# Levels of a triangular inverse as 32x32 products on four row groups in place of 64x64 products on two quadrants

## The reference

```python
a_mat = jnp.where(strict, jnp.einsum('bhnik,bhnjk->bhnij', k_beta, k) * decay, 0.0) + jnp.eye(C, dtype=f32)
tri = functools.partial(lax.linalg.triangular_solve, left_side=True, lower=True, unit_diagonal=True)
u = tri(a_mat, v * beta[..., None])
w = tri(a_mat, k_beta * jnp.exp(g)[..., None])
```

## Time and profile before

| | us |
|---|---|
| three runs | 1550.43, 1552.90, 1553.49 |
| median | 1552.90 |
| the profiled execution | 1550.74 |
| its span in the trace | 1548.3 |

### The profile page before, as it was taken

The page is one execution under the profiler, slowest core; times in us unless marked ns, Lnnn a source line. Parts: engine busy times, 40 slices in busy tenths (PEclk is TensorE's granted clock), DMA queues, the critical chain, the costliest instruction groups (busy, mean ns, idle before and its releaser), DMA issues.

```text
span 1548.3 us, 24568 instructions
## 1 busy us (share of the span) xinstructions
PE 1446.0 (93%) x10321; PEld 1158.1 (75%) x10321; DVE 682.0 (44%) x1063; ACT 605.1 (39%) x872; POOL 572.3 (37%) x265
## 2 busy tenths in 40 slices
PE   7999899888769999999999799987999999999998
PEld 5787578777758788888888687754467888888886
DVE  4665676777554312213143405877823413132231
ACT  5525463434344423223133335467844313232231
POOL 5343231101023434343434332326944443434441
PEclk9999898999869999999999899998999999999999
DMA  4332110000113232323233222210012232223231
GB/s 141 95 96 68 55 28 3 3 3 3 57 43 95 82 109 82 109 82 106 84 101 90 67 83 69 82 55 1 1 55 83 98 93 93 97 86 104 83 106 55
DMA packets 128392, 110.00 MB, mean 71 GB/s; under 512 B 10678, under 2 KB 126512, under 8 KB 128304
## 3 DMA queue, kind: packets, MB, share of 16 engines
q1 hardware_dynamic: 127712, 107.64, 22.4%
q10 hardware_dynamic: 592, 1.07, 0.2%
HBM read 106.60 MB, written 2.10 MB: 70 GB/s over the span
## 4 chain that ended last, share of the span: by engine, by line
PE 78%; DVE 11%; ACT 5%; issue 3%; POOL 2%; DMA 1%; DVEq 0%; ACTq 0%; SPq 0%; POOLq 0%
PE ps L501 21%; PE ps L506 21%; PE ps L502 21%; PE ps L637 5%; DVE lower L1874 2%; DVE lower L1870 1%; POOL lower L2083 1%; PE ps L652 1%; PE ps L645 1%; PE ps L741 1%; ACT lower L1371 1%; PE ps L614 1%; PE ps L538 1%; PE ps L948 1%; DVE lower L1653 1%
## 5 line engine op out<-in xcount | busy, mean ns | idle before, releaser
L2051 POOL TENSOR_TENSOR w_lo<-lower,w_hi 128x2048 fp32r<-128x2048 f32 x84 | 387.4, 4612 | 637.2 <-ACT w_hi L1027 637.2
L501 PE MATMUL ps<-h_hi,w_hi 128*128 128x512 f32 x792 | 315.9, 399 | 8.9 <-ACT h_hi L1032 5.9
L502 PE MATMUL ps<-h_hi,w_lo 128*128 128x512 f32 x792 | 314.5, 397 | 0.0
L1027 ACT ACTIVATE w_hi<-lower 128x2048 fp32r<-128x2048 f32 x84 | 160.2, 1907 | 242.8 <-PE ps L506 242.8
L506 PE MATMUL ps<-h_lo,w_hi 128*128 128x512 f32 x792 | 201.6, 395 | 0.4
L502 PE MATMUL ps<-a_hi,w_lo 128*128 128x512 f32 x480 | 189.1, 394 | 0.0
L501 PE MATMUL ps<-a_hi,w_hi 128*128 128x512 f32 x480 | 189.1, 394 | 0.0
L501 PEld LDWEIGHTS ps<-h_hi,w_hi 128*128 128x128 f32 x792 | 150.3, 190 | 46.5 <-issue 11.5
L502 PEld LDWEIGHTS ps<-h_hi,w_lo 128*128 128x128 f32 x792 | 150.2, 190 | 36.0 <-issue 0.5
L506 PEld LDWEIGHTS ps<-h_lo,w_hi 128*128 128x128 f32 x792 | 148.7, 188 | 37.4 <-DVE h_lo L1576 1.8
L1819 DVE TENSOR_TENSOR lower<-lower,ps 128x512 f32<-128x512 f32 x64 | 44.0, 687 | 268.7 <-PE ps L506 268.7
(11 more groups left out here) (356 smaller groups left out, 1992.4 us busy)
## 6 DMA issues: line engine op xcount, KB each, us to landing
lower<-in_mlp_w_dram SPq DMA_DIRECT2D x64, 1024.0 KB, 5.4
lower<-in_ev_w_in_dram SPq DMA_DIRECT2D x30, 512.0 KB, 3.8
lower<-in_od_w_in_dram SPq DMA_DIRECT2D x10, 1024.0 KB, 5.0
lower<-in_ev_w_out_dram SPq DMA_DIRECT2D x4, 1024.0 KB, 5.1
lower<-in_od_w_out_dram SPq DMA_DIRECT2D x4, 1024.0 KB, 5.1
out_dram<-lower SPq DMA_DIRECT2D x4, 512.0 KB, 3.2
lower<-in_od_w_in_dram SPq DMA_DIRECT2D x6, 256.0 KB, 3.8
upper<-in_x_dram SPq DMA_DIRECT2D x1, 1024.0 KB, 7.8
```

The lines of the kernel that those rows point to most:

```text
L501: pe.matmul(o, wh, xh, start=(i_ == 0), stop=False)
L502: pe.matmul(o, wl, xh, start=False, stop=False)
L1027: act.activation(WH[:, u % 2, :, 0:w], RAW[:, u % 2, :, 0:w], ACT.Copy).then_inc(hi_ready, 1)
L2051: pool.tensor_tensor(WL[:, u % 2, :, 0:w], RAW[:, u % 2, :, 0:w], as_f32(WH[:, u % 2, :, 0:w]), ALU.subtract)\
```

## The change

A new helper, `quarters`, takes the place of `both_halves` in the two functions of the inverse's levels. For levels 0 to 3 it makes, for each head, four products of 32x32 by 32x32, one for each group of 32 partitions: rows i, output partitions i, with the diagonal 32x32 block of the head's matrix that lies there. These are 32 products per call. For level 4 it makes two products per head, one per chunk, 16 per call: for the product below, from rows 0 to 31 of a chunk to its output partitions 32 to 63, and for the joined one (`lower` False) from rows 32 to 63 to partitions 0 to 31. Each product starts and stops its own accumulation. The other calls of `both_halves`, the semaphores, the masks and the work of all other engines stay as they are.

```diff
+            def quarters(b, lev, mats, vals, lower):
+
+                for h_ in range(NH):
+                    j, q = h_ // 2, h_ % 2
+                    for i in range(4):
+                        here_ = i // 2 * 2
+                        if lev < LAST - 1:
+                            row, col, m_, n_ = i, i, i % 2, i % 2
+                        elif i % 2 == 0:
+                            row, col, m_, n_ = (here_, here_ + 1, 1, 0) if lower else (here_ + 1, here_, 0, 1)
+                        else:
+                            continue
+                        rows, cols = (slice(x * 32, x * 32 + 32) for x in (row, col))
+                        mm = pe.matmul(ps[cols, b, h_ * HD + n_ * 32:h_ * HD + n_ * 32 + 32],
+                                       mats[rows, j, q, m_ * 32:m_ * 32 + 32], vals[rows, j, q, n_ * 32:n_ * 32 + 32],
+                                       start=True, stop=True)
+                return mm
+
             def below_blocks(s, lev):
...
-                    both_halves(g, lt, ti, True).then_inc(inv_x, 1)
+                    quarters(g, lev, lt, ti, True).then_inc(inv_x, 1)
...
                     if lev < LAST - 1:
-                        both_halves(g, qi[s % 2], xm, True).then_inc(inv_y, 1)
+                        quarters(g, lev, qi[s % 2], xm, True).then_inc(inv_y, 1)
                     else:
-                        both_halves(g, xm, qi[s % 2], True).then_inc(inv_y, 1)
+                        quarters(g, lev, xm, qi[s % 2], False).then_inc(inv_y, 1)
```

## The result

| | before | after |
|---|---|---|
| median of the runs on one chip, us | 1552.8 | 1597.0 (1593.7 to 1601.2) |
| ratio, 95% interval | | 1.0295 [1.0265, 1.0325] |
| the profiled execution, us | 1550.7 | 1598.6 |
| its span, us | 1548.3 | 1596.6 |

The change costs 44 us by the medians and 48 us between the two profiled executions. The stage table of the kernel after (same columns as the earlier trace rows) says where: round 0, rounds 1 to 3, the last round, and everything behind the stage.

A forecast was written before the change was run, and what follows sets the result against it. TensorE was taken to bound levels 0 and 1 and the last level's end, DVE level 2 and much of level 3. Terms -3.8 - 9.3 + 4.2 = -8.9 us gave 1544 against the median; forecast 1538 to 1551, range to 1580.

The forecast's parts named there:

- the burst: After a stall, four matmuls and five weight loads of L629 started within 60 ns; taken as showing fast enough issue.
- g, the price of a group: One matrix kind of one level, below or joined: from 0.93 us to 0.51 us, 64 passes on four tiles.
- rival 1: Levels 0 to 3: passes can't be issued or don't overlap fast enough; +46 us, 1599; chance 0.22 with milder forms.
- Round 0: First round of the chunk stage: level 0 gives -2.0, levels 1 to 3 up to -0.9 each; about -3.8 us.
- Rounds 1 to 3: Later rounds: shorter waits in levels 0, 1 and the last give -3.2 us a round, -2.9 in round 3.
- the clock's term: Rounds 1 to 3: one more slow stretch a round from idle TensorE gives back +1.4 us each, +4.2 in all.
- hidden under that: Level 2 in rounds 1 to 3: its products stay covered by DVE's own 5.9 us of work, so no gain.
- −1.1: Last level, rounds 1 and 2: products at the lower clock take half of 3.3 us, until DVE's L1606 is later.
- Rival 2: The clock falls through most of the stage: +2.5 us a round, -2 for round 0, about 1559; chance 0.12.
- Rival 3: Only two tiles overlap, a group takes 1.02 us and a level 4.1: 1554, no difference; chance 0.14.
- The floor of 25 ns: Skill page: starts never closer than about 25 ns however small the product, so 1.6 us a group.
- the serialization by bank: Skill page: different row tiles can't access one PSUM bank at once, so a group takes 2.0 us; given little weight.

The follow-up runs named there:

- two_of_four: Kernel after, but levels 0 to 3 multiply only blocks 0 and 2 of each matrix, so its result isn't the reference's; 1554.5 us, 1.0022 of before.
- loop_quarters: Kernel after with levels 1 to 3 as a hardware loop on TensorE, same products; 1576.4 us, 1.0159 of the kernel before.
- last_only: Kernel before with the 32x32 products in level 4 only, levels 0 to 3 unchanged; 1558.7 us, 1.0048 of before.
- filled_last: Kernel before with 32x32 products in level 4 only, plus products nobody reads where TensorE waits; 1551.2 us, 1.0008 of before.
- filled_more: Kernel before plus products nobody reads where TensorE waits, also in round 0 and more in the last round; 1542.4 us, 0.9948 of before.

## Why the prediction was wrong

**The step that failed** is "I take the burst as the better witness, since in every sustained stretch the tiles themselves account for the 29 ns". The runs showed a supply of 27 ns a pass in its place. The burst spent, by that, instructions that were already there after a stall. The sustained rate looked like the tiles' own only because the two limits nearly meet: 58 ns on two tiles is 29 ns a pass, and 256 instructions every 3.5 us are 27 ns a pass. A cause that accounts for a rate doesn't exclude a second limit right behind it. The rows could have shown it: the chain's 128 passes of a level held exactly one block of the instruction queue, one every 3.8 us (the DMA row of the kernel before, above), and the prediction doesn't read that queue.

**g, the price of a group.** Forecast 0.51 us at full clock, upper end 1.87. The array's part was nearly right, 0.6 us. As a sustained price a group is 128 instructions, half a block, so 1.75 us, close to the upper end. Four groups are 7.0 us, close to rival 1's 7.5 us a level (measured 6.9 to 7.2). Rival 1 was the right case for nearly the reason it gives ("Passes can't be issued, or don't overlap, fast enough"); it priced the whole at +46, and the medians say +44. The prediction gave it 0.22, milder forms included, and ended its range at 1580, below the rival's full price. That was too little: passes had to start less than 14.6 ns apart through a whole level for the rival not to decide, and no row showed that.

**Round 0.** Forecast −3.8; in the kernel after it is 8.8 us longer. two_of_four, with all but one of the pauses gone, has −3.5, but that it is so close is luck. Its levels run at the lower clock, so a group takes some 0.9 us (64 passes, two groups, in 1.92 us) and not 0.51, and copy to copy is 3.65 us where the forecast has 2.98:

```profile
243.48 1.92 PE L710 MATMUL ps<-lower,upper 32*32 32x32 f32 x64
244.59 1.58 DVE L1673 COPY_PREDICATED lower<-lower,ps 128x512 f32<-128x512 int32 x2 [0.89 <-PE ps L710]
248.25 1.58 DVE L1673 COPY_PREDICATED lower<-lower,ps 128x512 f32<-128x512 int32 x2 [0.31 <-PE ps L710]
```

Level 0 gives 2.4 us of the 3.5 (2.9 from first product to first copy, before 5.3); levels 1 to 3 give 0.4 where 2.2 was forecast, and 0.5 lies ahead of the levels. The third trip of loop_quarters has neither pauses nor the lower clock (1.00 from 254.3 to 257.8), and copy to copy is still 3.49 us there: 0.4 less than before, not 0.9. Of the half microsecond over the forecast, 0.3 stand before the joined product at 257.04 (rows above). The profile ends that wait with DVE's second transpose, which the forecast had under the chain; the loop's register waits stand at the same place, and these rows don't tell them apart.

**Rounds 1 to 3.** Forecast −3.2 +1.4 each; two_of_four, with no pauses, has +2.5. The forecast is 4.3 us a round too low even there. I put most of that down to the clock's term: I expected one more slow stretch, and 30 us of each of these rounds of two_of_four are at the lower clock. Level 2, "hidden under that", would have to fit under DVE's own 5.9 us; with two blocks at 3.5 us to wait for it is too long for that. In last_only, shorter products gain nothing at all in level 4: I put −1.1 there, and its rounds are 3.3 us longer.

**Rival 2** (the clock through most of the stage, 1559) described the clock rightly, and its price was of the right size: it forecast +6, and two_of_four, which is that case, has +3. It was not the larger cause. **Rival 3** (only two tiles overlap) needs 16 ns a pass at full clock and is excluded by the 10.

**The pages.** Four tiles start a pass every 13.3 ns at the lower clock, over 1 us, and every 10 ns at the upper. The floor of 25 ns between starts ("TensorE: Matmul & The Clock Gate" of the Trainium skill, section "Wait — 56ns, not 53.3ns?") is thus not seen between tiles. Its 1.6 us a group was nearer to the measured 1.75 than my 0.51, for another reason. All four row groups wrote one bank, at 0.6 us a group; the serialization by bank of the Trainium skill's "TensorEngine Tiling (Array Packing)" (section "Restrictions and Gotchas", an estimate of 2.0 us) isn't seen.

**What stays open:** how much of the cost that no pause explains (all 7 us of last_only, 7 of the 25 of loop_quarters) is the clock's; what the 3.5 us between blocks are made of (a transfer is some 1 us of them); how many blocks are held ahead (at least two, since loop_quarters' body of 512 instructions was not fetched again); and why the clock falls at the end of filled_last's rounds.

## What to carry to other kernels

Cutting a product into smaller ones multiplies instructions: before doing so, divide the instructions of a level by 256 and multiply by 3.5 us, and compare that with what the level takes, for one engine's straight-line code; the row of the instruction queue in the DMA view gives the count. A burst after a stall is no witness of a rate that must last. Where a short stage is bound by dependences and its clock sags, a few products that nothing needs, in PE's waits, can be worth more (−8 us here) than faster products (+44).

## What the hardware showed that was not expected

- Instructions of PE in straight-line code: blocks of 16 KB, 256 instructions, starts never closer than 3.3 us in the stage of any of these kernels; pauses of mostly 1.2 to 2.0 us when PE uses them up sooner. Repeated trips of a loop of 512 instructions bring no transfer and no pause of that size.
- Four 32x32 tiles of float32 run side by side into one bank: at 1.2 GHz 13.3 ns a pass, which is 53 ns for each tile, where a 64x64 tile takes 58 ns at 2.4 GHz. At 2.4 GHz it is 10 ns over 1.3 us, not half of 13.3; what holds it there is open.
- Less work can cost and more can pay, and what moves with it is the clock: two_of_four has the same times of ACT and DVE as before, fewer columns for PE, and 138 us at the lower clock in place of 49; filled_more has more work and 3.
